# Places of their own for the next stage's first weights at the norms of a two-layer fp32 diffusion step

## Chip, cores and metric

One core of a Trainium2 chip. The time is the device time of one execution in microseconds (us), the median of the runs. Engines: PE multiplies matrices, DVE is the vector engine, ACT the scalar engine, POOL the third elementwise engine, SP only issues transfers.

## What is computed

Two layers over two streams of 128 tokens (stream 0 the context, stream 1 the latent tokens), model width 2048, all in fp32. Each layer is an attention and gating mixer and a feed-forward block, both between two norms:

```python
def ffn_sublayer(x, shift, scale, gate, g_pre, g_post, w_gate, w_up, w_down):
    h = rms_norm(x, g_pre) * (1 + scale) + shift
    f = (jax.nn.silu(h @ w_gate) * (h @ w_up)) @ w_down
    return x + gate * rms_norm(f, g_post)
...
    for l in range(DEPTH):
        sm, cm, gm, sf, cf, gf = modulation(c_ctx, mod_w[l], mod_b[l])
        h = rms_norm(xp, norm_mix_pre[l]) * (1 + cm) + sm
        ...
        xp = xp + gm * rms_norm(merge_heads(o_a, o_b, o_c, w_out[l]), norm_mix_post[l])
        xp = ffn_sublayer(xp, sf, cf, gf, norm_ffn_pre[l], norm_ffn_post[l], w_gate[l], w_up[l], w_down[l])
```

`modulation` is one product of a conditioning vector with `mod_w` (2048 x 12288 for each layer), whose weights have to be read too. Matrices are 2048 x 4608 (`w_in`), 2048 x 2048 (`w_out`), 2048 x 5632 (`w_gate`, `w_up`) and 5632 x 2048 (`w_down`).

## The kernel before

**Pieces and chunks.** Weights come from HBM in pieces of 256 rows x 512 columns (512 KB). A *chunk* is 512 output columns: eight pieces, k = 0 to 15 in blocks of 128 rows, two blocks a piece. All pieces of the program are numbered: the first OUT stage is 72 to 103, the feed-forward stage behind it begins at 104, `w_in` of layer 1 at 368, the second feed-forward stage at 472. For each piece SP issues the transfer to `raw` (`piece`, line 502; once the piece four earlier is split), ACT casts it to `whi` (fp32r), DVE subtracts to `wlo`, and PE multiplies, for each block and stream, `lo x whi`, `hi x wlo`, `hi x whi` of 128 x 512 (12 matmuls a piece, 96 a chunk). `raw`, `whi`, `wlo` are rings of `RING` = 4 places; ACT and DVE may write a place of `whi` and `wlo` when the piece four earlier is used. `ahead` (line 1066) makes them split `LEAD` = 4 pieces in front of PE.

**Stages.** `w_in` in (in), attention, OUT (4 chunks), then three groups of gate/up chunks each with a down stage. Every engine has its own hand-written order, and semaphores tie them.

**The norm** (`turnover`, ACT line 1156, DVE line 1453) stands three times between two stages and, shorter, at the end. The last chunk before it runs its last four pieces for stream 0 first and then for stream 1 (`last=APART` in `dense`, line 747); `half_done` says that stream 0 is complete. Then, for stream 0: ACT copies the last columns out of the bank and squares them, DVE multiplies by the gate row (`gated`), takes the mean, POOL the power, DVE adds to x in four parts, ACT squares those, DVE and POOL make the next norm's factor, DVE normalises blocks of 512 columns to `f`, PE turns each (`turn_x`, four transposes to bank X), ACT or DVE scales by the modulation (`xtmp`), ACT casts to `xt_hi` and DVE subtracts to `xt_lo`. Between these stand the splits of the next stage's first four pieces, which need the ring's places, and stream 1's like work. The first chunk of the next stage (`first=APART`) takes pieces 0 to 3 for stream 0, then for stream 1, then 4 to 7 for both; `TURN_AT` says at which block which turn stands.

**The modulation of later stages** runs beside OUT: `OUT_MODS` gives the pieces after which PE does a *burst* (eight 32-row products over four pieces of `mod_w` in `mraw`, a ring of four), `OUT_FETCH` the pieces behind which SP issues their transfers in pairs. The last burst, ACT's copy of the row, PE's turn of it (`mod_tail`, bank T) and DVE's `norm_vectors` stand in the norm behind OUT. In the feed-forward stages DVE accumulates other vectors piece by piece (`acc`).

Of the kernel before, what the change touches and what calls it, by code (L numbers as in the profile page):

```python
# [56 lines left out]
def turn_order(l, which):  # L57

    if l == which == 0:
        return [(s, b) for b in range(ND) for s in range(2)]  # L60
    return [(0, 0), (0, 1), (1, 0), (1, 1), (0, 2), (1, 2), (0, 3), (1, 3)]


TURN_AT = {((0,), 5): (2, 3), ((1,), 1): (4,), ((1,), 3): (5,), ((1,), 6): (6,), ((0, 1), 8): (7,)}


def scaled_by_act(l, which, i):

    return i % 2 == 1 if l == which == 0 else i in (0, 2, 5, 7)


def edge_of(l, which):
# [209 lines left out]
def build_program(nc, a):  # L282
# [8 lines left out]
    with ExitStack() as ctx:  # L291
# [112 lines left out]
        dve_own = sem("dve_own")  # L404
        pool_own = sem("pool_own")
# [24 lines left out]

        def vec(v, l):
# [21 lines left out]
        def xt_count(l, which):  # L453


            return 16 * l + 8 * (which + 1)
# [281 lines left out]
        def _(pe):  # L738
# [8 lines left out]
            def dense(u, pair, i, hi, lo, nk=KD, ph=0, ready=None, m=None, behind={}, first=0, last=0):  # L747
# [6 lines left out]
                for js in (range(first), range(first, n - last), range(n - last, n)):  # L754
                    together = js.start == first and js.stop == n - last
                    for streams in [(0, 1)] if together else [(0,), (1,)]:
                        for j in js:
                            if streams[0] == 0:
                                pe.wait_ge(lo_ready, u * UNIT + (ph + j + 1))
                            slot = (ph + j) % RING  # L760
                            for kb in range(KB):
# [26 lines left out]
            def products(pair, k, hi, lo, slot, kb, nk=KD, first=0, last=None, streams=(0, 1)):  # L788
                for s in streams:
                    t = slice(s * P, (s + 1) * P)  # L790
                    for n, (xs, ws_) in enumerate([(lo, whi), (hi, wlo), (hi, whi)]):
                        mm = pe.matmul(bank[f"{pair}{s}"][:], xs[:, k, t], ws_[:, slot, kb, :],  # L792
# [4 lines left out]
            def start():  # L797
# [7 lines left out]
                for q in range(ND * QUARTER):  # L805
# [10 lines left out]
                    for kb in range(KB):  # L816
                        mm = products(pair, j * KB + kb, xt_hi, xt_lo, q % RING, kb, first=4 * n, last=4 * n + 3)
# [70 lines left out]
            def pre(l, which):  # L888


                done = xt_count(l, which) - 8

                def ready(k, streams):
# [3 lines left out]
                    if k % 4 == 0:  # L897
                        pe.wait_ge(xt_ready, done + {(0,): 1 + k // 4, (1,): 3 + k // 4, (0, 1): 2 + k // 2}[streams])
# [942 lines left out]
```

## Time and profile before

| what | value |
|---|---|
| runs | 2449.19, 2445.62, 2443.11 us; median 2445.62 |
| profiled execution | 2445.17 us, span 2443.4 |
| PE busy | 2310.0 us, 95% |
| DVE busy | 1578.3 us, 65% |
| ACT busy | 984.4 us, 40% |
| mean granted clock of PE | 0.975 |
| DMA | 609.93 MB, mean 250 GB/s |
| casts and subtractions of pieces | 736 of each, 1050 and 1223 ns |

Busy shares average over stages. The span counts from the first to the last instruction; the 1.8 us between it and the execution's own time lie around it. The three norms lie at 504 to 549, 1276 to 1321 and 1675 to 1720 us, the OUT stages at 412 to 511 and 1582 to 1681.

### The profile page before, as it was taken

To read this page: it belongs to the slowest core of one execution; us is meant where nothing else is said; L and a number is where in the kernel's file an instruction comes from. 1 tells how busy PE (TensorE), PEld (TensorE's weight loads), DVE (VectorE), ACT (ScalarE), POOL (GpSimd) and SP (SyncE) were. 2 spreads that over 40 slices of the span, in tenths; PEclk is the share of its full clock that TensorE was granted. 3 is DMA by queue.
4 is the path that set the end of the run, shared out by engine and by line. 5 is a ranking of instruction groups with operands and counts; after the bars stand their busy time and mean duration, and the time that the engine had idled before them with its cause. 6 is when DMAs were issued, how large, how long until landed. Compare 5 with 4: busy or idle time off the path is not lost.

```text
span 2443.4 us, 28114 instructions
## 1 busy us (share of the span) xinstructions
PE 2310.0 (95%) x10780; PEld 1806.2 (74%) x10780; DVE 1578.3 (65%) x1715; ACT 984.4 (40%) x1253; POOL 67.5 (3%) x97
## 2 busy tenths in 40 slices
PE   4999878989999999999998998798999999999998
PEld 1776645768878888788776885576888888878886
DVE  2555444479988889889886454446888644554455
ACT  2333232454444444334345344335444444434443
POOL 1000020000000000000000102000000000000000
PEclk8999988999999999999999999999999999999999
DMA  8779978858878878788864766885877666656664
GB/s 302 254 281 340 332 274 288 303 193 303 284 254 299 288 265 293 246 280 289 298 198 155 215 208 233 286 300 197 278 268 252 220 196 189 189 182 192 191 221 147
DMA packets 269319, 609.93 MB, mean 250 GB/s; under 512 B 19117, under 2 KB 19297, under 8 KB 267841
## 3 DMA queue, kind: packets, MB, share of 16 engines
q1 hardware_dynamic: 264832, 589.37, 71.5%
q0 software_dynamic: 4352, 18.76, 2.2%
q8 instruction: 86, 1.41, 0.2%
q14 instruction: 49, 0.39, 0.0%
HBM read 603.79 MB, written 5.45 MB: 249 GB/s over the span
## 4 chain that ended last, share of the span: by engine, by line
PE 84%; DMA 6%; DVE 4%; issue 2%; ACT 2%; SPq 0%; POOL 0%; DVEq 0%; POOLq 0%; ACTq 0%
PE bank_A L792 39%; PE bank_B L792 38%; DMA mraw<-in_mod_w 6%; PE bank_M L852 3%; PE bank_X L880 2%; DVE wlo L1362 1%; PE bank_M L841 1%; ACT whi L1094 1%; PE bank_T L872 1%; DVE xtmp L1443 1%; DVE x L1475 0%; DMA raw<-in_w_out 0%; DVE acc L1384 0%; PE bank_M L782 0%; ACT xtmp L1137 0%
## 5 line engine op out<-in xcount | busy, mean ns | idle before, releaser
L1362 DVE TENSOR_TENSOR wlo<-raw,whi 128x1024 fp32r<-128x1024 f32 x736 | 896.7, 1223 | 687.2 <-ACT whi L1094 687.0
L1094 ACT CAST whi<-raw 128x1024 fp32r<-128x1024 f32 x736 | 770.3, 1050 | 1190.8 <-PE bank_A L792 591.3
L792 PE MATMUL bank_A<-whi,xt_lo 128*128 128x512 f32 x1136 | 452.1, 398 | 17.9 <-DVE xt_lo L1413 11.1
L792 PE MATMUL bank_A<-wlo,xt_hi 128*128 128x512 f32 x1136 | 446.8, 393 | 0.0
L792 PE MATMUL bank_A<-whi,xt_hi 128*128 128x512 f32 x1136 | 446.5, 393 | 0.0
L792 PE MATMUL bank_B<-whi,xt_lo 128*128 128x512 f32 x1104 | 433.4, 393 | 0.5 <-issue 0.5
L792 PE MATMUL bank_B<-wlo,xt_hi 128*128 128x512 f32 x1104 | 430.0, 389 | 0.0
L792 PE MATMUL bank_B<-whi,xt_hi 128*128 128x512 f32 x1104 | 429.7, 389 | 0.0
L1384 DVE SCALAR_TENSOR_TENSOR acc<-mraw,cond,acc 128x1024 f32<-128x1024 f32 x300 | 371.2, 1279 | 0.0
L792 PEld LDWEIGHTS bank_A<-whi,xt_lo 128*128 128x128 f32 x1136 | 215.9, 190 | 84.5 <-issue 28.1
L792 PEld LDWEIGHTS bank_A<-whi,xt_hi 128*128 128x128 f32 x1136 | 215.8, 190 | 46.0
L792 PEld LDWEIGHTS bank_B<-whi,xt_lo 128*128 128x128 f32 x1104 | 207.3, 188 | 56.2 <-issue 13.4
L792 PEld LDWEIGHTS bank_A<-wlo,xt_hi 128*128 128x128 f32 x1136 | 215.9, 190 | 43.5
L792 PEld LDWEIGHTS bank_B<-whi,xt_hi 128*128 128x128 f32 x1104 | 207.2, 188 | 43.6
L792 PEld LDWEIGHTS bank_B<-wlo,xt_hi 128*128 128x128 f32 x1104 | 207.3, 188 | 42.0
L792 PE MATMUL bank_A<-whi,ht_lo 128*128 128x512 f32 x352 | 139.2, 395 | 0.7 <-DVE wlo L1362 0.7
L792 PE MATMUL bank_A<-wlo,ht_hi 128*128 128x512 f32 x352 | 138.3, 393 | 0.0
L792 PE MATMUL bank_A<-whi,ht_hi 128*128 128x512 f32 x352 | 137.9, 392 | 0.0
L792 PE MATMUL bank_B<-whi,ht_lo 128*128 128x512 f32 x352 | 137.5, 391 | 0.2 <-DVE wlo L1362 0.2
L792 PE MATMUL bank_B<-wlo,ht_hi 128*128 128x512 f32 x352 | 137.0, 389 | 0.0
L792 PE MATMUL bank_B<-whi,ht_hi 128*128 128x512 f32 x352 | 137.0, 389 | 0.0
L852 PE MATMUL bank_M<-mraw,cond 128*32 128x512 f32 x640 | 93.4, 689 | 30.7 <-DMA mraw<-in_mod_w 30.7
(193 smaller groups left out, 1432.9 us busy)
## 6 DMA issues: line engine op xcount, KB each, us to landing
mraw<-in_mod_w SPq DMA_DIRECT2D x384, 512.0 KB, 6.0
raw<-in_w_gate SPq DMA_DIRECT2D x176, 512.0 KB, 4.4
raw<-in_w_up SPq DMA_DIRECT2D x176, 512.0 KB, 4.4
raw<-in_w_down SPq DMA_DIRECT2D x176, 512.0 KB, 4.8
raw<-in_w_in SPq DMA_DIRECT2D x144, 512.0 KB, 4.7
raw<-in_w_out SPq DMA_DIRECT2D x64, 512.0 KB, 5.8
gate_mix<-gate_rows POOLq DMA_DIRECT2D x4, 1024.0 KB, 6.6
gate_ffn<-gate_rows POOLq DMA_DIRECT2D x4, 1024.0 KB, 9.0
```

What stands on the lines that cost most here:

```text
L792: mm = pe.matmul(bank[f"{pair}{s}"][:], xs[:, k, t], ws_[:, slot, kb, :], start=(k == first and n == 0), stop=(k == (nk - 1 if last is Non ...
L841: mm = pe.matmul(bank["M"][g:g + 32, :], cond[:, 2 * k:2 * k + 32], mraw[:, j % RING, kb, :], start=(k < 4), stop=(k >= KD - 4))
L852: mm = pe.matmul(bank["M"][32 * c:32 * c + 32, :], cond[:, 2 * k:2 * k + 32], mraw[:, ring_piece(m, j + c // 2) % RING, c % 2, :], start=( ...
L872: mm = pe.matmul(bank["T"][:, w * t:w * t + w], mrow[:, t * P:(t + 1) * P], sel[:], start=True, stop=True)
L880: mm = pe.transpose(bank[b][:, n * P:(n + 1) * P], t, ident[:])
L1094: act.copy(whi[:, ph % RING], raw[:, ph % RING]).then_inc(hi_ready, 1)
L1362: dve.tensor_tensor(wlo[:, ph % RING], raw[:, ph % RING], whi[:, ph % RING].bitcast(F32), ALU.subtract).then_inc(lo_ready, 1)
L1384: ins = dve.scalar_tensor_tensor(out=acc[:, h, s, :], in0=w, scalar=c, in1=acc[:, h, s, :], op0=ALU.mult, op1=ALU.add)
L1443: ins = dve.tensor_scalar(xtmp[:, b % 2, s, t, :], bank[bk][:, t * P:(t + 1) * P], scal[:, k, s:s + 1], shift[:, k, s:s + 1], ALU.mult, AL ...
```

## The change

- Places (`EXTRA`, `weights`, `place_free`): the next stage's first four pieces at each norm don't go to the ring but to memory of the feed-forward block that is idle there: halves of `ht_lo` or `ht_hi`, `w_hid` (over `hid` and `sil`) and `w_acc` (over `acc`). The ring's pieces behind them then wait for the piece eight earlier (`last_use`).
- `ahead` splits these four before the norm's chain begins; the four splits inside `turnover` are now those of pieces 4 to 7.
- The first chunk runs all eight pieces for stream 0, then all for stream 1 (`first=UNIT`), with turns in the order of the streams.
- Block 0 of stream 0 is scaled, cast and subtracted in halves (`pre_halves`); ACT scales all blocks but one.
- Behind OUT, squares and gate products read the bank directly, with no copy to `f` first; in all norms the mean stands ahead of the last gate product.
- The modulation's six bursts now all stand inside OUT, with their turn and vectors (`OUT_TAIL`), and `OUT_MODS` and `OUT_FETCH` have new piece numbers.

```diff
-    return [(0, 0), (0, 1), (1, 0), (1, 1), (0, 2), (1, 2), (0, 3), (1, 3)]
-
...
-TURN_AT = {((0,), 5): (2, 3), ((1,), 1): (4,), ((1,), 3): (5,), ((1,), 6): (6,), ((0, 1), 8): (7,)}
+    return [(s, b) for s in range(2) for b in range(ND)]
...
-    return i % 2 == 1 if l == which == 0 else i in (0, 2, 5, 7)
+    return i % 2 == 1 if l == which == 0 else i != 2
...
-OUT_MODS = {3: (0, range(0, 4)), 8: (0, range(4, 8)), 13: (1, range(0, 4)), 19: (1, range(4, 8)), 24: (2, range(0, 4))}
+OUT_MODS = {3: (0, range(0, 4)), 8: (0, range(4, 8)), 12: (1, range(0, 4)), 17: (1, range(4, 8)),
+            21: (2, range(0, 4)), 25: (2, range(4, 8))}
 OUT_FETCH = {4: (0, (0, 1)), 5: (0, (2, 3)), 11: (0, (4, 5)), 12: (0, (6, 7)), 16: (1, (0, 1)), 17: (1, (2, 3)),
-             22: (1, (4, 5)), 23: (1, (6, 7)), 27: (2, (0, 1)), 28: (2, (2, 3)), 31: (2, (4, 5, 6, 7))}
+             20: (1, (4, 5)), 21: (1, (6, 7)), 25: (2, (0, 1)), 26: (2, (2, 3)), 29: (2, (4, 5)), 30: (2, (6, 7))}
+OUT_TAIL = 26
+EDGE_PIECE = [104, 368, 472]
+EXTRA = {g + e: (edge, e) for edge, g in enumerate(EDGE_PIECE) for e in range(RING)}
+
+
+def last_use(g):
+
+    return g - RING if g - RING not in EXTRA else g - 2 * RING
+
+
 MOD_PE = [2, 3, 4, 9, 10]
...
+        with ExitStack() as until_acc:
+            w_acc = sb("w_acc", [P, 4, KB, CH], F32R, until_acc)
...
+        with ExitStack() as until_hid:
+            w_hid = sb("w_hid", [P, 2, KB, CH], F32R, until_hid)
...
+        def weights(g):
+
+            if g not in EXTRA:
+                return whi[:, g % RING], wlo[:, g % RING]
+            edge, e = EXTRA[g]
+            if edge % 2:
+                places = [(tiles(ht_hi, 12), tiles(ht_lo, 12)), (w_hid[:, 0], w_hid[:, 1]),
+                          (w_acc[:, 0], w_acc[:, 1]), (w_acc[:, 2], w_acc[:, 3])]
+            else:
+                places = [(tiles(ht_lo, 0), tiles(ht_lo, 4)), (tiles(ht_lo, 8), tiles(ht_lo, 12)),
+                          (w_hid[:, 0], w_hid[:, 1]), (w_acc[:, 2], w_acc[:, 3])]
+            return places[e]
+
+        def place_free(engine, g):
+
+            if g in EXTRA:
+                if EXTRA[g] in ((1, 2), (1, 3)):
+                    engine.wait_ge(acc_read, MOD_DVE.index(8) + 1)
+            elif g >= RING:
+                engine.wait_ge(w_used, last_use(g) + 1)
...
-            return 16 * l + 8 * (which + 1)
+            return 8 + 9 * (2 * l + which)
...
-                done = xt_count(l, which) - 8
+                done = xt_count(l, which) - 9
...
-                    if k % 4 == 0:
-                        pe.wait_ge(xt_ready, done + {(0,): 1 + k // 4, (1,): 3 + k // 4, (0, 1): 2 + k // 2}[streams])
+                    if streams == (0,) and k in (0, 2):
+                        pe.wait_ge(xt_ready, done + 1 + k // 2)
+                    elif k % 4 == 0:
...
-                    dense(i * 2 + u, "A", i + use["A0"], xt_hi, xt_lo, ready=ready, first=APART if ready else 0)
+                    dense(i * 2 + u, "A", i + use["A0"], xt_hi, xt_lo, ready=ready, first=UNIT if ready else 0)
...
+                        if i == ND - 1 and k == KB * (OUT_TAIL % UNIT + 1):
+                            mod_tail(m + MOD_OUT)
...
+            def pre_halves(l, which):
+
+                bk, n = plan.at[(l, "pre_uses", which)][0]
+                fill_of(bk, n)
+                for k in range(4):
+                    ins = act.activation(xtmp[:, 0, 0, k, :], bank[bk][:, k * P:(k + 1) * P], ACT.Identity,
+                                         scale=scal[:, k, 0:1], bias=shift[:, k, 0:1])
+                    if k == 1:
+                        ins.then_inc(act_own, 1)
+                        act.wait_ge(act_own, edge_of(l, which))
+                        high(xt_hi[:, 0:2, 0:P], xtmp[:, 0, 0, 0:2])
+                ins.then_inc(freed[bk], 1)
+                act.wait_ge(freed[bk], n + 2)
+                high(xt_hi[:, 2:4, 0:P], xtmp[:, 0, 0, 2:4])
+
...
+                def last_square(s):
+                    if which:
+                        act.wait_ge(freed[f"B{s}"], use[f"B{s}"] + 3)
+                        return f_square(s, n)
+                    if s:
+                        act.wait_ge(w_used, u * UNIT + ph + pieces)
+                    else:
+                        act.wait_ge(half_done, edge_of(l, which) + 1)
+                    square(bank[f"B{s}"][:], ssq[:, s, n:n + 1])
...
+                last_square(0)
...
+                ahead = ph + pieces + LEAD
+                split(u, ahead)
+                x_squares(0, range(ND))
+                last_square(1)
...
+                pre_halves(l2, w2)
+                pre_block(l2, w2, 1)
+                x_squares(1, range(2))
...
+                x_squares(1, range(2, ND))
+                pre_block(l2, w2, 3)
+                split(u, ahead + 2)
+                split(u, ahead + 3)
+                for i in range(4, 8):
+                    pre_block(l2, w2, i)
...
-                    ahead(split, u, late=lambda j: pre_late(l, 0, j))
+                    ahead(split, u, LEAD, UNIT - LEAD)
...
+                        ahead(split, u + i, 0, 2)
+                        mod_row(m + MOD_OUT)
+                        ahead(split, u + i, 2, UNIT - 2)
+                        turnover(l, 0, u + i, 0, UNIT, use, split)
...
-                            ahead(split, u, 2 * n * i, 2 * n, leave=LEAD if i == ND - 1 else 0)
+                            ahead(split, u, 2 * n * i, 2 * n)
...
+                mean_square(ssq, sq + 7, slice(0, 1))
                 gated(l, which, ND - 1, 0, sq + 7)
...
+                ahead = ph + pieces + LEAD
+                l2, w2 = l + which, 1 - which
...
+                normal(l2, w2, 2, 3)
...
+                pre_low(l2, w2, 0, range(2))
...
+                add(1, [0])
+                pre_low(l2, w2, 0, range(2, 4))
+                add(1, [1])
+                pre_scale(l2, w2, 2)
+                pre_low(l2, w2, 1)
+                add(1, [2, 3])
+                pre_low(l2, w2, 2)
+                split(u, ahead + 1)
...
+                split(u, ahead + 2)
+                split(u, ahead + 3)
+                normal(l2, w2, 6, 7)
+                for i in range(4, 8):
+                    pre_low(l2, w2, i)
...
+                        ins = dve.tensor_tensor(f[:, i, c], bank[b][:], gate_mix[:, i, c], ALU.mult)
+                        ins.then_inc(freed[b], 1)
...
+                ahead(split, u + ND - 1, 0, 3)
+                mod_cols(m + MOD_OUT)
+                norm_vectors(l, 1)
+                ahead(split, u + ND - 1, 3, UNIT - 3)
+                turnover(l, 0, u + ND - 1, 0, UNIT, split)
```

The order of ACT at the first norm, from the last OUT pieces' casts on; before:

```order
L1094 CAST whi<-raw 128x1024 x4
L1166 COPY f<-bank_B 128x512
L1108 ACTIVATE junk,ssq<-f 128x512
L1094 CAST whi<-raw 128x1024 x2
L1108 ACTIVATE junk,ssx<-x 128x512 x4
L1108 ACTIVATE junk,ssq<-f 128x512
L1123 COPY mrow<-bank_M 128x512
L1094 CAST whi<-raw 128x1024 x2
L1137 ACTIVATE xtmp<-bank_X,shift,scal 128x128 x4
L1112 CAST xt_hi<-xtmp 128x4x128
```

and now:

```order
L1132 CAST whi<-raw 128x1024 x2
L1132 CAST ht_lo<-raw 128x1024 x2
L1132 CAST w_hid<-raw 128x1024
L1132 CAST w_acc<-raw 128x1024
L1146 ACTIVATE junk,ssq<-bank_B 128x512
L1132 CAST whi<-raw 128x1024
L1146 ACTIVATE junk,ssx<-x 128x512 x4
L1146 ACTIVATE junk,ssq<-bank_B 128x512
L1132 CAST whi<-raw 128x1024
L1200 ACTIVATE xtmp<-bank_X,shift,scal 128x128 x2
L1150 CAST xt_hi<-xtmp 128x2x128
L1200 ACTIVATE xtmp<-bank_X,shift,scal 128x128 x2
```

Four more casts (to `ht_lo`, `w_hid`, `w_acc`) stand ahead of the square of the last chunk, its copy is gone, and the row's copy (`mrow`) has moved ahead of them.

The order of DVE at the same place; before:

```order
L1362 TENSOR_TENSOR wlo<-raw,whi 128x1024 x4
L1587 TENSOR_TENSOR f<-f,gate_mix 128x512
L1407 TENSOR_REDUCE msum<-ssq 128x1
L1408 TENSOR_SCALAR ms<-msum 128x1
L1475 SCALAR_TENSOR_TENSOR x<-f,rstd,x 128x512 x4
L1470 COPY f<-bank_B 128x512
L1362 TENSOR_TENSOR wlo<-raw,whi 128x1024
L1407 TENSOR_REDUCE msum<-ssx 128x1
L1408 TENSOR_SCALAR ms<-msum 128x1
L1587 TENSOR_TENSOR f<-f,gate_mix 128x512
L1407 TENSOR_REDUCE msum<-ssq 128x1
L1408 TENSOR_SCALAR ms<-msum 128x1
```

and now:

```order
L1419 TENSOR_TENSOR wlo<-raw,whi 128x1024
L1419 TENSOR_TENSOR ht_lo<-raw,ht_lo 128x1024 x2
L1419 TENSOR_TENSOR w_hid<-raw,w_hid 128x1024
L1419 TENSOR_TENSOR w_acc<-raw,w_acc 128x1024
L1462 TENSOR_REDUCE msum<-ssq 128x1
L1463 TENSOR_SCALAR ms<-msum 128x1
L1640 TENSOR_TENSOR f<-bank_B,gate_mix 128x512
L1527 SCALAR_TENSOR_TENSOR x<-f,rstd,x 128x512 x4
L1419 TENSOR_TENSOR wlo<-raw,whi 128x1024
L1462 TENSOR_REDUCE msum<-ssx 128x1
L1463 TENSOR_SCALAR ms<-msum 128x1
L1484 TENSOR_SCALAR f<-x,rstd 128x512 x2
```

The subtractions of the four early pieces come first, the mean has changed places with the gate product, and the copy to `f` is gone.

The order of SP in the OUT stage, from the pair of `mod_w` pieces behind piece 17 on; before:

```order
L500 DMA mraw<-in_mod_w 128x1024 x2
L506 DMA raw<-in_w_out 128x2x512 x5
L500 DMA mraw<-in_mod_w 128x1024 x2
L506 DMA raw<-in_w_out 128x2x512
L500 DMA mraw<-in_mod_w 128x1024 x2
L506 DMA raw<-in_w_out 128x2x512 x4
L500 DMA mraw<-in_mod_w 128x1024 x2
L506 DMA raw<-in_w_out 128x2x512
L500 DMA mraw<-in_mod_w 128x1024 x2
L506 DMA raw<-in_w_out 128x2x512 x3
L500 DMA mraw<-in_mod_w 128x1024 x4
L506 DMA raw<-in_w_gate 128x2x512 x5
```

and now:

```order
L541 DMA mraw<-in_mod_w 128x1024 x2
L547 DMA raw<-in_w_out 128x2x512 x3
L541 DMA mraw<-in_mod_w 128x1024 x2
L547 DMA raw<-in_w_out 128x2x512
L541 DMA mraw<-in_mod_w 128x1024 x2
L547 DMA raw<-in_w_out 128x2x512 x4
L541 DMA mraw<-in_mod_w 128x1024 x2
L547 DMA raw<-in_w_out 128x2x512
L541 DMA mraw<-in_mod_w 128x1024 x2
L547 DMA raw<-in_w_out 128x2x512 x3
L541 DMA mraw<-in_mod_w 128x1024 x2
L547 DMA raw<-in_w_out 128x2x512
```

The pairs stood behind pieces 17, 22, 23, 27 and 28 and four pieces behind 31; now they stand behind 17, 20, 21, 25, 26 and 29 (and 30, in the row after the last one).

## Rows read from the trace of the kernel before

**Rows 1.** The page: the chain that ended last, by engine.

```profile
PE 84%; DMA 6%; DVE 4%; issue 2%; ACT 2%; SPq 0%; POOL 0%; DVEq 0%; POOLq 0%; ACTq 0%
```

**Rows 2.** The chain of waits in order of time: start, us, what.

```profile
454.14 1.85 PE bank_M L852 x16
...
488.30 1.85 PE bank_M L852 x16
...
504.06 0.60 ACT f L1166
...
549.25 21.76 PE bank_B L792 x96
...
1278.44 0.79 PE bank_T L872 x8
```

**Rows 3.** Timeline of PE, 518 to 549: start, us, engine, line, operation [idle before].

```profile
518.19 0.77 PE L792 MATMUL bank_A<-whi,xt_lo 128*128 128x512 f32 x1 [2.55 <-DVE xt_lo L1413]
518.75 0.63 PE L792 MATMUL bank_A<-wlo,xt_hi 128*128 128x512 f32 x1
519.18 0.63 PE L792 MATMUL bank_A<-whi,xt_hi 128*128 128x512 f32 x1
...
549.09 0.39 PE L792 MATMUL bank_B<-whi,xt_lo 128*128 128x512 f32 x1
```

**Rows 4.** Timeline of ACT, 504 to 517.

```profile
504.68 0.63 ACT L1108 ACTIVATE junk<-f 128x512 f32<-128x512 f32 x1
...
514.88 1.50 ACT L1137 ACTIVATE xtmp<-bank_X,shift,scal 128x128 f32<-128x128 f32 x4 [0.55 <-PE bank_X L880]
516.42 0.62 ACT L1112 CAST xt_hi<-xtmp 128x512 fp32r<-128x512 f32 x1
```

**Rows 5.** Timeline of DVE, 505 to 546.

```profile
505.43 0.69 DVE L1587 TENSOR_TENSOR f<-f,gate_mix 128x512 f32<-128x512 f32 x1 [4.46 <-ACT junk L1108]
...
507.19 2.74 DVE L1475 SCALAR_TENSOR_TENSOR x<-f,rstd,x 128x512 f32<-128x512 f32 x4 [0.68 <-POOL rstd L650]
...
513.12 0.88 DVE L1429 TENSOR_SCALAR f<-x,rstd 128x512 f32<-128x512 f32 x2
...
544.50 1.41 DVE L1381 TENSOR_SCALAR acc<-mraw,cond 128x1024 f32<-128x1024 f32 x2
```

**Rows 6.** Operations of a tile by stretch: 446, 480, 499 to 512, 1274; issue and landing.

```profile
L500 SPq DMA_DIRECT2D mraw<-in_mod_w x1: 430/430/430, 446.6 to 446.6; - x1
...
DMA to landing us min/median/max: 6.7/6.7/6.7
...
L500 SPq DMA_DIRECT2D mraw<-in_mod_w x1: 431/431/431, 480.8 to 480.8; - x1
...
DMA to landing us min/median/max: 7.1/7.1/7.1
...
L1094 ACT CAST whi<-raw x1: 1048/1048/1048, 498.7 to 498.7; 128x1024 fp32r<-128x1024 f32 x1
L1362 DVE TENSOR_TENSOR wlo<-raw,whi x1: 1226/1226/1226, 499.8 to 499.8; 128x1024 fp32r<-128x1024 f32 x1
...
L506 SPq DMA_DIRECT2D raw<-in_w_gate x2: 368/368/368, 501.0 to 511.7; - x2
...
DMA to landing us min/median/max: 3.6/4.0/4.3
...
L506 SPq DMA_DIRECT2D raw<-in_w_in x1: 367/367/367, 1274.1 to 1274.1; - x1
...
DMA to landing us min/median/max: 4.6/4.6/4.6
```

**Rows 7.** Timelines of PE and DVE at the second norm, 1275 to 1321.

```profile
1290.00 0.76 PE L792 MATMUL bank_A<-whi,xt_lo 128*128 128x512 f32 x1 [2.27 <-DVE xt_lo L1413]
...
1320.98 0.39 PE L792 MATMUL bank_B<-whi,xt_lo 128*128 128x512 f32 x1
...
1275.76 0.69 DVE L1468 TENSOR_TENSOR f<-f,bank_B 128x512 f32<-128x512 f32 x1
```

More of the change, by code:

```diff
@@ L786, in dve_vector, with products @@
                     vector_turn(vector_tail(MOD_TAIL[g]), rsel4)
-            def products(pair, k, hi, lo, slot, kb, nk=KD, first=0, last=None, streams=(0, 1)):
+            def products(pair, k, hi, lo, g, kb, nk=KD, first=0, last=None, streams=(0, 1)):
+                w_hi, w_lo = weights(g)
                 for s in streams:
                     t = slice(s * P, (s + 1) * P)
-                    for n, (xs, ws_) in enumerate([(lo, whi), (hi, wlo), (hi, whi)]):
-                        mm = pe.matmul(bank[f"{pair}{s}"][:], xs[:, k, t], ws_[:, slot, kb, :],
+                    for n, (xs, w) in enumerate([(lo, w_hi), (hi, w_lo), (hi, w_hi)]):
+                        mm = pe.matmul(bank[f"{pair}{s}"][:], xs[:, k, t], w[:, kb, :],
                                        start=(k == first and n == 0),
@@ L816, in start @@
                     for kb in range(KB):
-                        mm = products(pair, j * KB + kb, xt_hi, xt_lo, q % RING, kb, first=4 * n, last=4 * n + 3)
+                        mm = products(pair, j * KB + kb, xt_hi, xt_lo, q, kb, first=4 * n, last=4 * n + 3)
                     mm.then_inc(w_used, 1)
@@ L1061, in _, with ahead @@
                               last=APART if g == len(GROUPS) - 1 and i == ND - 1 else 0)
-        def ahead(split, u, ph=0, pieces=UNIT, between=None, leave=0, late=None):
-            for j in range(pieces - leave):
+        def ahead(split, u, ph=0, pieces=UNIT):
+            for j in range(pieces):
                 split(u, ph + LEAD + j)
-                if late:
-                    late(j)
-                if between and j == pieces - 1 - max(leave, 1):
-                    between()
         def past_end(u, ph):
@@ L1091, in split @@
                 act.wait_ge(raw_landed[ph % RING], u * (16 * UNIT // RING) + 16 * (ph // RING + 1))
-                if not (isinstance(u, int) and u * UNIT + ph < RING):
-                    act.wait_ge(w_used, u * UNIT + (ph - RING + 1))
-                act.copy(whi[:, ph % RING], raw[:, ph % RING]).then_inc(hi_ready, 1)
+                place_free(act, u * UNIT + ph)
+                act.copy(weights(u * UNIT + ph)[0], raw[:, ph % RING]).then_inc(hi_ready, 1)
                 if u * UNIT + ph in MOD_ROW:
@@ L1311, in hidden_high @@
                                      four(bank[f"X{s}"][:])).then_inc(ht_hi_ready, 1)
[L1313 removed]
+                    ahead(split, u, 0 if g else LEAD, UNIT if g else UNIT - LEAD)
                     silu(u, 0, True)
@@ L1714, in pair @@
                 def pair(i):
-                    ahead(split, i * 2 + u, late=None if i else lambda j: pre_late(l, 0, j))
+                    ahead(split, i * 2 + u, 0 if i else LEAD, UNIT if i else UNIT - LEAD)
                     read_out(i * 2 + u, i * 2 * CH, "A")
@@ L1760, in _ @@
                     first = 2 * (FFC * l + c0)
-                    ahead(split, u, late=None if g else lambda j: pre_late(l, 1, j))
+                    ahead(split, u, 0 if g else LEAD, UNIT if g else UNIT - LEAD)
                     for i in range(0, n - 1):
@@ L1779, in _ @@
                         else:
-                            ahead(split, u, 2 * n * i, 2 * n, leave=LEAD if i == ND - 1 else 0)
+                            ahead(split, u, 2 * n * i, 2 * n)
                             if i:
```

136 lines of the change are left out of this document (43 added, 93 removed).

## Prediction

> **What bounds the kernel now.** I read the page's chain first: matmuls carry 84% of it [rows 1]. A chunk of 96 dense matmuls takes 21.76 us, 2.72 us for a piece [rows 2], and nothing in the change touches their number. What can move is PE's idle time, so I went through the chain in order of time and stopped where PE is not the link: at the three norms between stages, and in front of the bursts of modulation products. At the first norm the last chunk's stream 0 is complete at 504.06 [rows 2]. The next stage's first dense matmul starts at 518.19 and its second chunk at 549.09 [rows 3]: 14.13 us, then 30.90 us for a chunk whose matmuls need 21.76. The third norm repeats this within 0.1 us. At the second, stream 0 is complete at 1275.76, and the two marks are 1290.00 and 1320.98 [rows 7].
>
> **What goes.** In that 14.13 us PE runs a burst (1.85 us) and the vector's turn (0.79 us where it stands between dense matmuls) [rows 2]. Both move ahead of the mark, into the OUT stage. PE still does them, so this term is a transfer: 2.64 us leave the norm and 2.64 us enter the stage. Reading the bank directly drops ACT's copy. Taking the mean before the gate product hides 0.69 us of gating behind the power: DVE's gating starts at 505.43 and its additions at 507.19, 1.76 us later, of which 0.68 is the wait for POOL [rows 5]. By the new order this is 0.37 (mean) + 0.75 (gate beside power) = 1.12 us.
>
> **What is added to the norm.** ACT and DVE now cast and subtract four pieces of the next stage ahead of the chain. The last of them can be issued only when the last OUT piece is split. In the trace that issue is at 501.0, 3.06 us ahead of the mark, and it landed after 4.3 us; the one issued into an idle queue took 3.6 [rows 6]. The four modulation pieces that queued ahead of it now go out two OUT pieces earlier, so I take 3.6: landed at mark + 0.54. Cast 1.05 [rows 6] gives + 1.6, the square of the last chunk (0.63 and its read-out, about 0.75) [rows 4] + 2.35, DVE's subtraction 1.23 [rows 6] + 2.8. So the chain starts 2 us late, by work that stood behind it before. From there: mean 0.37, gate beside power 0.75, + 3.9; first addition 0.75 and four squares of ACT at 0.82, + 7.95; mean 0.35 and power 0.65, + 8.95; first normalised block 0.45 (0.88 for two [rows 5]), + 9.4; four transposes at the low clock 1.1, + 10.5; half of ACT's scaling (1.50 for four [rows 4]) 0.8, + 11.3; half a cast, between 0.31 (half of 0.62 [rows 4]) and 0.62, taken at 0.4, + 11.7; half a subtraction, likewise 0.4, + 12.15. The first dense matmul starts 12.15 us after the mark in place of 14.13.
>
> **The first chunk.** 96 matmuls are 21.8 us. Twelve run at the low level: starts at 518.75 and 519.18 are 0.43 us apart against 0.23 at the high one [rows 2, 3], 2.4 us. PE had been idle 2.55 us ahead of the first [rows 3]; it will be idle again, so I keep the twelve. Six turns between matmuls cost 0.45 each, 2.7. That is 26.9; the trace's 30.90 holds 4.0 us of waits, since stream 0's first half is followed at once by stream 1's and pieces are split between blocks. With all eight pieces at hand and stream 0 whole, I walked the engines forward: PE waits 0.35 for the seventh piece's subtraction, and 0.85 for stream 1's first block, because the first accumulation (1.41 us on DVE [rows 5]) stands ahead of that block's normalisation. With 0.25 for smaller ones: 28.35. The norm after an OUT stage gives 1.98 + 2.55 - 2.64 = 1.9 us, and two of them 3.8.
>
> **The second norm** is less kind. The down stage's last chunk has six pieces, and the last early one can be issued only after the chunk's own last split, at 1274.1; it takes 4.6 us to land [rows 6], 1278.7. Cast and subtraction end at 1280.95. Gating of chunk 2 (two like that in [rows 5]), the four short vector operations and the last addition, which began at 1275.76 [rows 7], come behind them on DVE: 1.3 + 0.5 + 0.65, 1283.4. The same chain from there (0.75 + 0.37 + 0.75 + 4.03 + 0.6 + 0.65 + 0.45 + 1.13 + 0.8 + 0.45 + 0.4) gives the first dense matmul at 1293.8, 3.8 us later than 1290.00. The chunk then takes 27.5 (no accumulation in it) in place of 30.98. Net +0.3 us.
>
> **The end** has the gate/power exchange twice, 0.62 each by the like of [rows 5]: 1.25 us gained.
>
> **The bursts in OUT.** They move from after pieces 3, 8, 13, 19, 24 and the stage's end to 3, 8, 12, 17, 21, 25, and the transfers for them to behind pieces 17, 21, 26 and 30. A raw piece q is issued when q-4 is split, so after q-8 is used. The burst after 13 was fed behind 17: four pieces of lead. The bursts after 12 (fed behind 17), 21 (26) and 25 (30) have three. In the trace the last transfer for the burst after 13 was issued at 446.6 and landed 6.7 us later, 453.3 [rows 6]; the burst began at 454.14 [rows 2]. One piece earlier its second half wants that data at 454.14 - 2.72 + 0.93 = 452.35: 0.95 short. For the burst after 24 the transfer was issued at 480.8 and took 7.1, 487.9 [rows 6]; the burst began at 488.30 [rows 2]; one piece less gives 486.5, 1.4 short. Chunk 1's boundary gets lighter, so the first takes 0.9, the others 1.4: 3.7 us a stage, 7.4 us in two. Nothing hides them, PE waits. Bounds: 0 (landings as fast as at the norm) and 2.4 a burst (one piece's lead, nearly whole), 0 to 14.4.
>
> What the pair of transfers costs is where a page speaks otherwise. The Trainium skill, "DMA: Bandwidth & Descriptors", section "Anatomy of one DMA — SWDGE (gpsimd) path", fits about 2.0 us plus bytes over 436 GB/s: 3.2 us for 512 KB. The rows' 6.7 and 7.1 are transfers behind others in the queue, the 3.6 at the norm is near the page. By the page's price alone all bursts would be fed in time and the sum would be the first rival's.
>
> **The sum,** against the profiled execution's own 2445.17 us (span 2443.4): -3.8 + 0.3 - 1.25 + 7.4 = +2.65, 2447.8. The median of the runs shown is 2445.62, within half a microsecond; I say 2448.
>
> **Rivals.** (a) *The bursts are fed in time.* The modulation pairs are spread more evenly, so that each queues behind less. Then 7.4 falls away: 2440.5. For it: the 3.6 us landing. Against it: pairs at 446 and 480 were not crowded either. (b) *Fed in time, and the clock is back sooner.* PE's pause at a norm gets shorter; if only half of the twelve matmuls run at the low level and the transposes too, about 1.7 us less at each of three norms: 2435.5. For it: the pause ahead of the first matmul; against: after a 2.55 us pause all twelve were slow. (c) *Slower: every shifted burst waits nearly a whole piece,* 2.4 us for six: 2454.8. It decides the sign beyond measurement above 2.0 us a burst. The longest latency that supports it is 7.1. (d) *The early splits cancel the norm's gain:* the fourth piece lands after 6 us instead of 3.6 at all three norms, the chain starts that much later: 2447.8 + 3.8 = about 2452. The change then does not do what its name says.
>
> **How the numbers follow.** Forecast 0.40, (a) 0.23, (b) 0.15, (c) 0.12, (d) 0.10. A measurement tells about 0.3%, 7.3 us, from no change: faster is below 2438.3, slower above 2453.0. Faster holds (b) and the lower edge of (a): 0.20. Slower holds (c) and the upper edge of (d) and of the forecast: 0.16. Same 0.64. The range leaves out part of (b) and the top of (c): 2436 to 2455.
>
> **What would show it.** In the new profile: PE waits for the modulation tile's transfers in both OUT stages, near 1 us at three bursts each; first dense matmul about 12 us behind the first mark and 18 behind the second; the first chunk 28 us; waits of the first chunk's matmuls for split weights gone but one. No wait at the bursts proves (a); a mark-to-matmul time near 14 proves (d). I would be wrong altogether if a wait came up that the trace doesn't have, for example in the second chunk, whose pieces can be split only as the ring frees in stream 1's pass.

## Result: 11 us slower, and the profile after

The changed kernel takes 2457.24 us (median of 10 runs, 2449.00 to 2463.88); the kernel before, run beside it, 2445.90 (10 runs, 2442.82 to 2451.14). The ratio of the two is 1.0049, 95% interval 1.0036 to 1.0063: slower by 11 us or half a percent, outside the range of the prediction and within 2.5 us of its rival (c).

The profiled execution of the changed kernel took 2461.3 us (span 2459.5), 16.1 us over the span before. Its chain has less of PE and more of DMA than [rows 1]:

```profile
PE 81%; DMA 8%; DVE 5%; ACT 2%; issue 2%; SPq 1%; POOL 1%; POOLq 0%; DVEq 0%; ACTq 0%
L893 PE MATMUL bank_M<-mraw,cond 128*32 128x512 f32 x640 | 92.3, 674 | 44.2 <-DMA mraw<-in_mod_w 44.1
```

The last row is the page's group of all modulation products: duration, mean ns, and 44.2 us of idle time ahead of them, nearly all of it waiting for transfers. The same row of the kernel before has 30.7 us, none of it inside an OUT stage:

```profile
L852 PE MATMUL bank_M<-mraw,cond 128*32 128x512 f32 x640 | 93.4, 689 | 30.7 <-DMA mraw<-in_mod_w 30.7
```

I cut both spans at five marks that each chain of waits shows: the first dense matmul of each OUT stage and the start of the second chunk behind each norm. The stretches add up to the spans, and so their differences to 16.1.

| stretch | before | after | difference | predicted |
|---|---|---|---|---|
| start to first OUT stage | 411.59 | 411.29 | -0.3 | 0 |
| first OUT stage and first norm | 137.66 | 145.32 | +7.7 | +1.8 |
| feed-forward and second norm | 771.89 | 772.45 | +0.6 | +0.3 |
| `w_in` and attention of layer 1 | 261.12 | 262.52 | +1.4 | 0 |
| second OUT stage and third norm | 137.69 | 145.05 | +7.4 | +1.8 |
| rest, with the end | 723.45 | 722.87 | -0.6 | -1.25 |

The loss lies in the OUT stages. These are the waits there, from the timeline of PE (start, us, operation, idle time before it and what ended it), first stage, then second:

```profile
440.63 1.07 PE L893 MATMUL bank_M<-mraw,cond 128*32 128x512 f32 x8 [0.61 <-DMA mraw<-in_mod_w]
...
456.01 1.07 PE L893 MATMUL bank_M<-mraw,cond 128*32 128x512 f32 x8 [2.20 <-DMA mraw<-in_mod_w]
...
487.11 1.06 PE L893 MATMUL bank_M<-mraw,cond 128*32 128x512 f32 x8 [2.23 <-DMA mraw<-in_mod_w]
...
502.87 1.06 PE L893 MATMUL bank_M<-mraw,cond 128*32 128x512 f32 x8 [1.01 <-DMA mraw<-in_mod_w]
...
1635.24 1.07 PE L893 MATMUL bank_M<-mraw,cond 128*32 128x512 f32 x8 [1.55 <-DMA mraw<-in_mod_w]
...
1666.40 1.07 PE L893 MATMUL bank_M<-mraw,cond 128*32 128x512 f32 x8 [2.30 <-DMA mraw<-in_mod_w]
...
1681.78 1.06 PE L893 MATMUL bank_M<-mraw,cond 128*32 128x512 f32 x8 [2.17 <-DMA mraw<-in_mod_w]
```

They are 6.05 and 6.02 us, where 3.7 a stage was predicted; the bursts of before in [rows 2] run their sixteen products in one go. Each stands in the middle of a burst, ahead of its second half. Two of them cost more than themselves: the dense matmuls behind the wait run at the lower of PE's two clock levels for a while.

```profile
488.10 0.64 PE L833 MATMUL bank_A<-whi,xt_lo 128*128 128x512 f32 x1
488.54 0.63 PE L833 MATMUL bank_A<-wlo,xt_hi 128*128 128x512 f32 x1
...
491.53 0.48 PE L833 MATMUL bank_A<-whi,xt_hi 128*128 128x512 f32 x1
491.85 0.40 PE L833 MATMUL bank_A<-whi,xt_lo 128*128 128x512 f32 x1
```

The starts are 0.43 us apart up to 491.5 and 0.23 to 0.32 from there. By the chain of waits those twelve took 4.55 us; twelve behind another stalled burst took 2.98:

```profile
441.69 2.98 PE bank_B L833 x12
...
488.17 4.55 PE bank_A L833 x12
```

### The profile page after: what moved, and what is told of

The parts are those of the page before. It is cut to its first block, busy times and chain, and to the rows that moved or that the text cites. A ratio compares the mean times of both kernels' runs of the same rounds, so it can differ in the third digit from the quotient of the medians.

```text
span 2459.5 us, 28085 instructions
## 1 busy us (share of the span) xinstructions
PE 2312.7 (94%) x10780; PEld 1808.9 (74%) x10780; DVE 1561.8 (64%) x1674; ACT 994.1 (40%) x1284; POOL 67.5 (3%) x97
## 4 chain that ended last, share of the span: by engine, by line
PE 81%; DMA 8%; DVE 5%; ACT 2%; issue 2%; SPq 1%; POOL 1%; POOLq 0%; DVEq 0%; ACTq 0%
PE bank_A L833 38%; PE bank_B L833 36%; DMA mraw<-in_mod_w 7%; PE bank_M L893 3%; PE bank_X L921 2%; DVE wlo L1419 2%; PE bank_M L882 1%; ACT whi L1132 1%; PE bank_T L913 1%; DMA raw<-in_w_out 0%; ACT junk L1146 0%; SPq L541 0%; DVE x L1527 0%; DVE xt_lo L1468 0%; DVE acc L1439 0%
## 5 line engine op out<-in xcount | busy, mean ns | idle before, releaser
L1419 DVE TENSOR_TENSOR wlo<-raw,whi 128x1024 fp32r<-128x1024 f32 x724 | 881.8, 1223 | 708.3 <-ACT whi L1132 707.6
L1132 ACT CAST whi<-raw 128x1024 fp32r<-128x1024 f32 x724 | 758.6, 1050 | 1201.9 <-PE bank_A L833 600.7
L833 PE MATMUL bank_A<-whi,xt_lo 128*128 128x512 f32 x1088 | 430.5, 396 | 4.2 <-DVE xt_lo L1468 3.7
L833 PE MATMUL bank_A<-wlo,xt_hi 128*128 128x512 f32 x1088 | 426.9, 392 | 0.0
L833 PE MATMUL bank_A<-whi,xt_hi 128*128 128x512 f32 x1088 | 426.2, 392 | 0.0
L833 PEld LDWEIGHTS bank_A<-whi,xt_lo 128*128 128x128 f32 x1088 | 206.3, 190 | 66.6 <-issue 22.5
L833 PEld LDWEIGHTS bank_A<-whi,xt_hi 128*128 128x128 f32 x1088 | 206.2, 190 | 43.7
L833 PEld LDWEIGHTS bank_A<-wlo,xt_hi 128*128 128x128 f32 x1088 | 206.3, 190 | 41.9
L833 PE MATMUL bank_A<-whi,ht_lo 128*128 128x512 f32 x352 | 138.8, 394 | 0.7 <-DVE wlo L1419 0.7
L833 PE MATMUL bank_A<-wlo,ht_hi 128*128 128x512 f32 x352 | 137.7, 391 | 0.0
L893 PE MATMUL bank_M<-mraw,cond 128*32 128x512 f32 x640 | 92.3, 674 | 44.2 <-DMA mraw<-in_mod_w 44.1
```

The costliest lines, as they stand in the source:

```text
L833: mm = pe.matmul(bank[f"{pair}{s}"][:], xs[:, k, t], w[:, kb, :], start=(k == first and n == 0), stop=(k == (nk - 1 if last is None else l ...
L893: mm = pe.matmul(bank["M"][32 * c:32 * c + 32, :], cond[:, 2 * k:2 * k + 32], mraw[:, ring_piece(m, j + c // 2) % RING, c % 2, :], start=( ...
L1132: act.copy(weights(u * UNIT + ph)[0], raw[:, ph % RING]).then_inc(hi_ready, 1)
L1419: dve.tensor_tensor(lo, raw[:, ph % RING], hi.bitcast(F32), ALU.subtract).then_inc(lo_ready, 1)
```

## Experiments

Theory after the result: the bursts with three pieces of lead are the whole loss, by their waits, and by the clock where a wait lowers it. Rivals: the bursts cost what the prediction said and the rest is in the norms; or traffic and the number of restarts cost, not the lead. All times below are medians beside runs of the kernel before on the same chip, 2445.53 for the first four kernels, 2445.86 for the last four. Beside the changed kernel it was 2445.90, so I subtract medians across the three series; by the scatter of the runs such a difference is known to about 4 or 5 us.

### The burst table alone, in the kernel before

```diff
-OUT_MODS = {3: ..., 8: ..., 13: (1, range(0, 4)), 19: (1, range(4, 8)), 24: (2, range(0, 4))}
+OUT_MODS = {3: ..., 8: ..., 12: (1, range(0, 4)), 17: (1, range(4, 8)), 21: (2, range(0, 4)), 25: (2, range(4, 8))}
...
-                mod(m + MOD_OUT, range(UNIT // 2, UNIT))
```

and `OUT_FETCH` as in the changed kernel.

> The kernel before with one part of the change: its modulation bursts in the OUT stages run after pieces 3, 8, 12, 17, 21 and 25 with the transfers moved to match; norms, chunk order and places are the old ones. In the changed kernel's trace the first OUT stage holds 6.05 us of waits for the modulation tile in five places, a chunk part at the low clock after one of them (4.55 us for twelve matmuls in place of 2.72) and four restarts at 2.98 us a piece in place of 2.72. Theory (the short leads and the clock that PE loses after such a wait are the whole loss): 6.05 + 1.8 + 1.0 = 8.9 us a stage, and 1.85 us more, because the last burst leaves a place at the norm where it was hidden: 2 x 10.75 = +21.5, about 2467 us. Rival (bursts cost the 3.7 us a stage of the prediction, the rest of the loss is in the norms): 2 x (3.7 + 1.85) = +11, 2457 us, with waits near 1 us at the bursts and no piece at the low clock.

Measured: 2461.72 us, ratio 1.0063 (1.0039 to 1.0087), +16.2. That lies between the two figures. The profiled execution, with span 2466.1, is 22.7 us over that of before. Its chain has the waiting transfers (these are of the first OUT stage) and a wait that the changed kernel avoids, PE waiting 3.0 us for ACT's copy of the row, since `mod_tail` still stands behind the stage:

```profile
446.76 7.50 DMA mraw<-in_mod_w
...
477.47 6.65 DMA mraw<-in_mod_w
...
491.64 7.50 DMA mraw<-in_mod_w
```

No low-clock piece followed a wait in the first OUT stage, the waits there being 4.7 us. In the second they are 5.6 us, and the last, 2.90 us, was followed by one: the 48 matmuls behind it took 12.73 us, the same 48 in the first stage 11.12.

```profile
1682.62 12.73 PE bank_B L794 x48
```

So a table of numbers, with none of the places or orders in the change's name, makes the kernel before slower by 16 us. The profile is with the theory and the medians lie midway, so this run alone doesn't decide between them; the later ones do.

### Bursts in pairs, evenly spread

```diff
+OUT_MODS = {q: (n // 4, (2 * n % 8, 2 * n % 8 + 1)) for n, q in enumerate([2, 4, 6, 8, 10, 12, 14, 17, 19, 21, 24, 25])}
+OUT_FETCH = {q: (n // 4, (2 * n % 8, 2 * n % 8 + 1)) for n, q in enumerate([4, 5, 10, 12, 14, 16, 18, 20, 22, 25, 27, 29])}
```

> The changed kernel, its six bursts of four modulation pieces cut into twelve of two, after pieces 2, 4, 6, 8, 10, 12, 14, 17, 19, 21, 24 and 25, each pair's transfer behind the piece that follows the pair two before it: every lead is four or five pieces, as many products as before. Theory: the waits in both OUT stages go, and with them the piece at the low clock: 2 x (6.05 + 1.8) = -16, 2441 us. Rival one (bursts cost 3.7 a stage): -7.4, 2450. Rival two (it is not the lead but the traffic: the latencies grow as transfers are spread, or twelve restarts of 0.25 us cost what the waits did): 2455 or more, with waits still there.

Measured: 2447.20 us, ratio 1.0004 (0.9987 to 1.0021), 10.0 less than the changed kernel. Both OUT stages have no wait for `mraw` at all (138.8 and 138.3 us with their norms, in place of 145.3 and 145.1). The -16 fell short by 6. A restart of dense matmuls behind a burst costs about 0.3 us whether the burst is of two or four pieces; with six more a stage that is 3.6 of the 6, and the rest is within the scatter. The rows are

```profile
423.69 1.00 PE bank_M L891 x8
424.69 5.67 PE bank_A L831 x24
```

where 24 matmuls need 5.44 and eight products 0.93.

### The last early pieces split behind the chain

```diff
+def held_back(l, which):
+    return 2 if which else 1
...
-                split(u, ahead)
+                rest = [ahead + e for e in range(-held_back(l, which), RING)]
+                split(u, rest[0])
                 x_squares(0, range(ND))
                 last_square(1)
-                split(u, ahead + 1)
+                split(u, rest[1])
```

and the like on DVE, where `rest[0]` stands behind `add(0)` and `rest[1]` behind `add(1, [1])`; the last chunk's `ahead` splits one or two pieces fewer.

> The changed kernel, but the early pieces that land last (the fourth at the norms after OUT, the third and fourth at the norm after the down stage) are split behind the last square and behind the first additions of the norm's chain in place of ahead of it. Places, transfers and products are the same. Theory (the splits hold the chain): the chain starts 2.0 us sooner at the first and third norm (mean at 518.97 in the trace, possible at about 516.9) and 4.3 us sooner at the second (last addition at 1289.15, possible at 1284.8), all of it kept since PE wants those pieces only 3 to 4 us into the chunk: -8.3, 2449 us. Rival (what is taken from the front comes back as waits of the first chunk for its split pieces or blocks): 2455 or more, and a first chunk longer than 28.4 us.

Measured: 2447.66 us, ratio 1.0008 (0.9991 to 1.0024), 9.6 less than the changed kernel. At the first norm stream 0 is complete at 508.53 (the end of its 36 matmuls) and the first dense matmul starts at 518.59, 10.06 us later in place of 12.22; the first chunk takes 28.20 in place of 28.43, so nothing is given back:

```profile
500.25 8.28 PE bank_B L838 x36
...
518.59 2.69 PE bank_A L838 x6
...
546.79 21.76 PE bank_B L838 x96
```

From the last down chunk to the second chunk behind the second norm it is 91.15 us in place of 93.74: 2.6 of the 4.3. The first dense matmul comes 61.4 us behind that down chunk's start in place of 65.9, the 4.3 expected; but the chunk takes 29.7 us (1288.33 to 1318.05) in place of 27.8, which is the rival, at this one norm. At the third norm mark to matmul is 10.07 us in place of 11.95. The three give 2.2 + 2.6 + 1.9 = 6.7. The profile also has shorter waits in OUT, 5.0 and 4.2 us, which the edit doesn't aim at, 2.8 us less than in the changed kernel; whether the other 2.9 of the 9.6 is that or scatter stays open.

### Both together

The two edits above in one kernel.

> The edits of the two kernels ahead of this one together: bursts in pairs, late pieces split behind the norm's chain. Theory: both gains add up, -16 and -8.3: 2433 us, 13 us faster than the kernel before. Rival (one gain hides the other, or the second is given back in the first chunk): 2441 or more.

Measured: 2435.28 us, ratio 0.9962 (0.9944 to 0.9981): -22.0 against the changed kernel, where 10.0 and 9.6 had been measured singly. They add up within the scatter, and the kernel is faster than the one before.

### One table altered: four pieces of lead

```diff
-             20: (1, (4, 5)), 21: (1, (6, 7)), 25: (2, (0, 1)), 26: (2, (2, 3)), 29: (2, (4, 5)), 30: (2, (6, 7))}
+OUT_FETCH = {4: (0, (0, 1)), 5: (0, (2, 3)), 11: (0, (4, 5, 6, 7)), 16: (1, (0, 1, 2, 3)), 20: (1, (4, 5, 6, 7)),
+             25: (2, (0, 1, 2, 3)), 29: (2, (4, 5, 6, 7))}
```

Nothing else of the changed kernel is touched.

> The changed kernel with one table altered: all four modulation pieces for a burst are issued behind one weight piece, the eighth after the burst before, so that each burst has four pieces of lead (the one after 17 five); bursts, places and norms as changed. Theory (the lead of three pieces is what the bursts pay for, not their number or size): nearly all of the waits in OUT and the low-clock piece go, without the six extra restarts a stage that bursts in pairs had (0.3 us each, 3.6 in all; that kernel took 2447.2): about 2443 to 2445 us. Rival (four transfers in a row land later by 0.8 us for each that stands ahead, and hold the weight pieces behind them): waits near 1 us stay at four bursts a stage, 2450 us or more.

Measured: 2442.17 us, ratio 0.9988 (0.9977 to 1.0000): 15.1 less than the changed kernel. This is the cleanest price of the bursts' lead, though its profiled execution (2450.29) was the slowest of its twelve. In that one the two stretches of OUT and norm take 139.6 and 137.6 us, together 13.2 less than in the changed kernel's. The waits of the first OUT stage are 0.6 us in one place, the second has none:

```profile
PE bank_M L893 <- DMA mraw<-in_mod_w: 0.6, 1, 0.6
```

although each transfer takes longer from issue to landing, four standing in a row (those issued at 454.4 and 454.9):

```profile
L541 SPq DMA_DIRECT2D mraw<-in_mod_w x2: 430/677/924, 454.4 to 454.9; - x2
...
DMA to landing us min/median/max: 9.0/9.4/9.8
```

The rival was right that they land later, and wrong on what it costs: 0.6 us in one place of two stages.

### One table altered: two pieces of lead

`OUT_FETCH` of the changed kernel with its last ten keys each one higher.

> The changed kernel with each of the ten moved transfers of the modulation pieces issued one weight piece later (leads of two in place of three; four in place of four or five at the others less one). Theory (a burst waits for landing less lead, and landing is near 7.9 us whatever the lead): each of four stalled bursts a stage waits 2.72 us more, the one with four pieces of lead begins to wait 2 us: 2 x (4 x 2.72 + 2) = +26, 2483 us, less what shorter queues give. Rival (what the transfer queues behind is the weight pieces, so a later issue lands sooner and the wait is capped near 2.3 us): under 2468 us.

Measured: 2497.86 us, ratio 1.0214 (1.0195 to 1.0234): +40.6 for one piece less of lead, where +26 was expected, and -15.1 for one piece more. The rival's cap falls. The first OUT stage with its norm takes 164.5 us. Idle time there:

```profile
PE bank_M L893 <- DMA mraw<-in_mod_w: 18.2, 8, 2.7
```

That is 12.1 over the changed kernel's 6.05, near the 13 expected. Most of the other 7 us of the stage's +19.2 is the clock, of which I had expected nothing more. The eight stalls are, in order, 2.41, 2.12, 2.72, 2.15, 1.79, 2.68, 1.65 and 2.67 us. Three of them, each the second stall within one burst, are followed by a burst at the low level (1.93 or 1.94 us for eight products in place of 1.07) and dense matmuls 0.43 us apart. The three bursts took 2.6 us longer for it and the dense matmuls behind them 4.3, where the changed kernel lost 1.6 in this stage; 1.2 us more went at the stage's entry (13.20 us for its first 48 matmuls in place of 12.01, see the last section). The rows of the first of the three:

```profile
456.76 1.93 PE L893 MATMUL bank_M<-mraw,cond 128*32 128x512 f32 x8 [2.72 <-DMA mraw<-in_mod_w]
458.62 0.80 PE L833 MATMUL bank_B<-whi,xt_lo 128*128 128x512 f32 x1
459.22 0.63 PE L833 MATMUL bank_B<-wlo,xt_hi 128*128 128x512 f32 x1
459.64 0.63 PE L833 MATMUL bank_B<-whi,xt_hi 128*128 128x512 f32 x1
```

Stretches by granted clock (the number ahead of the DMA share), behind two of these stalls:

```profile
456.76:465.91 9.15, 9.15 (x33) 6.11 (x34) 1.22 (x1) 1.05 (x1) 0.00 (x0) 0.72 0.16 60
514.60:521.07 6.47, 6.47 (x23) 3.93 (x23) 0.00 (x0) 0.59 (x1) 0.00 (x0) 0.59 0.29 108
```

The Trainium skill, "TensorE: Matmul & The Clock Gate", section "HAM oscillation — how this bites in real kernels", describes this: a wait for DMA between stretches of matmuls returns PE to its cold clock, and each stretch then pays for warming up on top of the wait; the waits of its example are longer than any of these. This trace agrees for three of the eight stalls; the five others, up to 2.41 us, were followed by full speed. In the second stage it agrees for four of eight (2.71, 2.71, 2.73 and 2.73 us).

### Four pieces of lead, late splits

The last altered table and `held_back` together.

> The early issue of the modulation pieces and the late split of the last early pieces together (bursts of four, leads of four). Theory: -9.6 (held back, as measured against the changed kernel) and -13: 2434 to 2436 us, level with the pairs and held-back kernel (2435.3) or 2 us under it, since twelve restarts are saved and four transfers in a row cost a part of that. Rival: waits near 1 us stay at the bursts: 2441 or more.

Measured: 2433.32 us, ratio 0.9956 (0.9942 to 0.9970). The lowest of all: 24 us under the changed kernel, 12.5 under the one before. The 2 us under the pairs and held-back kernel are within the scatter. The stretches are 134.5 and 133.2 us for OUT and norm, against 137.7 before. The second norm keeps the wait that holding back brings:

```profile
PE bank_A L838 <- DVE wlo L1426: 1.8, 1, 1.8
```

### Old norms, bursts in pairs

The kernel before with the pairs' two tables and nothing left at the stage's end. Against the pairs kernel it lacks the new norms, places, chunk order and end, and nothing else.

> The kernel before (its norms, chunk order and places) with the twelve bursts of two in OUT, fed with four pieces of lead, none left at the stage's end. It differs from the pairs kernel (2447.2 us) by the new norms, places, chunk order and end alone. By the traces: the last burst leaves its hidden place, 1.85 us, and six more restarts of 0.3: 2 x 3.65 = +7.3, 2453 us; the new norms would be worth about 6 us. By the prediction's own terms the chain and first chunk after OUT are worth 2 x 4.5 us, the end 1.25 and the second norm costs 0.3: this kernel would be 10 us slower than the pairs kernel, 2457. Rival (the new norms bring nothing): 2447.

Measured: 2455.75 us, ratio 1.0044 (1.0027 to 1.0060). The pairs kernel is 8.5 us faster. By this the rival (the new norms bring nothing) falls. Between the 6 of the expectation and the 10 of the prediction's own terms the runs don't decide. In the profiled executions the two stretches of OUT and norm are 145.8 and 142.7 us, against 138.8 and 138.3 in the pairs kernel; 2.3 of the 11.4 between them lie at the entry of the stages (last section). From the last down chunk to the second chunk behind the second norm the pairs kernel takes 2.0 us more, 94.5 against 92.6.

## Why the prediction was wrong

**The chain and chunk behind OUT: right.** Stream 0 complete to first dense matmul was predicted 12.15 us, the first chunk 28.35. At the first norm the mark (stream 0 complete) is 515.96 (510.52 and 24 matmuls, 5.44 us):

```profile
507.68 2.84 PE bank_B L833 x12
...
512.93 3.61 DMA raw<-in_w_gate
...
528.18 2.90 PE bank_A L833 x6
...
556.61 3.40 PE bank_B L833 x15
```

12.22 and 28.43 us. The fourth piece landed in 3.61 us (3.6 assumed), which ends rival (d) as it was put. That rival was right about one thing, though: the early splits do hold the chain. The prediction had priced that at 2 us, and it is 2.2 and 1.9, by the held-back kernel.

**The second norm: right mechanism, 0.9 us more than predicted.** Last down chunk to second chunk is 93.74 us against 92.56, +1.2 in place of +0.3. Its first dense matmul comes 4.5 us later than before, 3.8 predicted, and the chunk takes 27.8 in place of 27.5:

```profile
1280.80 4.35 DMA raw<-in_w_in
...
1287.39 1.30 DVE f L1637 x2
...
1301.25 2.90 PE bank_A L833 x6
```

**The end: 0.6 of 1.25 gained.** Gate and power now lie side by side twice, but POOL's power took 0.93 us in the last of them, against 0.56 before.

**The term that failed is the bursts': 7.4 predicted, 15.1 measured** (changed kernel less four-pieces-of-lead kernel), at the upper bound of 14.4 within the scatter. The mechanism was right, PE waiting for transfers whose lead had become three pieces; the size of the waits was wrong, and what they do to the clock was put at nothing. The identity of the stalled bursts was right (after 12, 21, 25), and so was their lead. In the changed kernel the last pair for the burst after 12 was issued at 448.02, and PE wanted it at 456.01 - 2.20 = 453.81: 5.79 us. The prediction's own numbers were 446.6 and 452.35: 5.75. For the burst after 21 it is 479.11 to 484.88, 5.77. With the 0.14 us from landing to product, a burst with three pieces of lead waits its landing time + 0.14 - 5.8. What was wrong:

- *The landing times.* I took 6.7 and 7.1 us from single transfers of before [rows 6] as though they went with the burst. They are 7.86, 7.86 and 6.67 in the first stage, 7.21, 7.95 and 7.83 in the second:

```profile
448.02 7.86 DMA mraw<-in_mod_w
...
479.11 7.86 DMA mraw<-in_mod_w
...
496.06 6.67 DMA mraw<-in_mod_w
```

  By this they give 2.2, 2.2, 1.0 and 1.55, 2.3, 2.2; with 0.61 at the burst after 8 that is 12.1 us for two stages, 4.7 over the forecast. The pair of 448.02 stood behind a weight piece that itself took 6.3 us; before, the one issued at 445.7 took 4.8. The rows, after and then before:

```profile
L547 SPq DMA_DIRECT2D raw<-in_w_out x1: 378/378/378, 447.1 to 447.1; - x1
...
DMA to landing us min/median/max: 6.3/6.3/6.3
```

```profile
L506 SPq DMA_DIRECT2D raw<-in_w_out x1: 379/379/379, 445.7 to 445.7; - x1
...
DMA to landing us min/median/max: 4.8/4.8/4.8
```

  So what stood ahead of the pair landed 1.5 us later, and I had priced each pair as if it met the backlog of before. Part of it is scatter: in the first OUT stage the kernel with the burst table alone has 7.50, 6.65 and 7.50 with the same spacing, and the held-back kernel 7.00, 7.33 and 7.68. The twelve together have a mean of 7.4, which by the same sum is 1.75 us a burst and 5.3 a stage, against 3.7. How much of the 7.4 comes from packing the same 24 transfers into fewer pieces wasn't tried.
- *What a wait does besides waiting.* The twelve matmuls at 488.17 took 1.57 us more than those at 441.69, and those at 1682.84 (4.54) likewise: 3.1 us. The prediction discussed the clock only at the norms. With the 12.1 us of waits, less the 0.6 that the kernel with four pieces of lead keeps, that is 14.6 of the 15.1.
- *The bound.* "One piece's lead, nearly whole" for three bursts a stage left out that the burst after 8, with four pieces, can be late (0.61 us), and left out the clock (3.1 us), so 14.4 was no real bound; the profiled execution has 12.1 + 3.1 = 15.2 us.

**The rivals.** Rival (c), 2454.8, had the right size for nearly the right reason (2.20, 2.23, 1.01 and 1.55, 2.30, 2.17 us at the six shifted bursts, the clock on top); I gave it 0.12 with the words that the longest latency that supports it is 7.1. [rows 6] are a handful of transfers and no maximum; the same trace of before has this pair, issued at the stage's end:

```profile
L500 SPq DMA_DIRECT2D mraw<-in_mod_w x2: 429/574/718, 490.2 to 490.7; - x2
...
DMA to landing us min/median/max: 8.7/9.1/9.5
```

Rival (a), the bursts fed in time, is the kernel with one table altered: 2442.17 for a forecast of 2440.5. The forecast's other terms thus stand within 2 us, and the 0.9 of the second norm and 0.65 of the end, missed above, are 1.55 of the 1.7. Rival (b) has no support. The first chunk's granted clock (the number ahead of the DMA share) is 0.92, and was 0.91, in these stretches of after and before:

```profile
528.18:556.61 28.43, 27.72 (x121) 21.97 (x122) 18.31 (x30) 21.44 (x46) 0.55 (x1) 0.92 0.30 97
```

```profile
518.19:549.09 30.90, 28.17 (x120) 21.81 (x121) 24.86 (x43) 17.14 (x32) 0.55 (x1) 0.91 0.55 178
```

Rival (d) was priced wrongly besides: a piece landing 2.4 us later at three norms would be 7.2 us, 2455.0, and not the 3.8 that were added.

A transfer's price was the place where the Trainium skill spoke otherwise ("DMA: Bandwidth & Descriptors", section "Anatomy of one DMA — SWDGE (gpsimd) path": about 2.0 us plus bytes over 436 GB/s, 3.2 us for 512 KB), in a fit to transfers issued by gpsimd, where these are issued by SP. The trace agrees within half a microsecond where nothing stood ahead, the fourth early piece at 3.61 us. The pair behind a weight piece took 7.1 and 7.9, and there the measurement decides: a lead is set by these.

```profile
L541 SPq DMA_DIRECT2D mraw<-in_mod_w x2: 433/450/467, 447.5 to 448.0; - x2
...
DMA to landing us min/median/max: 7.1/7.5/7.9
```

## What to carry to other kernels

A prefetch has a lead (from issue to need) and a landing time behind everything queued ahead of it. When a change moves the consumer one step earlier, work out the lead from the trace and hold it against the longest landing under load, not against one row: here one step less cost 15 us and the next 41, and one table that issues a step earlier gave the first back. Where a norm or another serial chain has a fixed start, put no work ahead of it that waits for a transfer still under way: moving one or two such splits behind the chain's first steps gave 9.6 us, 6.7 of them seen in the norms.

## What the runs showed of the hardware

**A stall of PE near 2 us may or may not lower its clock.** The length alone doesn't decide. In the changed kernel 2.20 and 2.30 us were followed by full speed, 2.17 and 2.23 by a stretch at the low level. With the late splits 2.03 us in the first OUT stage was followed by full speed, and 1.91 us in the second by the low level:

```profile
1650.69 1.07 PE L898 MATMUL bank_M<-mraw,cond 128*32 128x512 f32 x8 [1.91 <-DMA mraw<-in_mod_w]
...
1651.75 4.55 PE bank_A L838 x12
```

All eight waits in the OUT stages of 2.67 us or more were followed by the low level. Six of them stood behind an earlier stall of 1.65 to 2.12 us in the same burst, but 2.71 us (two pieces of lead, at 1638.73) and the 2.90 us of the burst table alone had no stall ahead of them in their burst. The longest alone that was followed by full speed is 2.41 us. What decides between 1.9 and 2.4 us stays open.

**The same instructions behind the same pause took different times.** Every kernel here has one pause in the middle of the feed-forward stage of layer 0, followed by the same 84 matmuls. In the profiled executions they took between 20.43 and 21.90 us, where 84 at full speed need 19.0:

```profile
985.48 20.48 PE bank_A L792 x84
```

The row is of the kernel before; this one is of the pairs kernel:

```profile
983.87 21.90 PE bank_A L831 x84
```

The entry of OUT is like it. The first 48 matmuls of its first stage took 11.1 us in the kernel before and in the one with four pieces of lead and late splits, in profiled executions, 12.01 in the changed one (12.39 in the second stage) and 12.42 with the burst table alone, whose program up to that point is that of before. About 2 us of the 16.1 in the table above are this and not the change, and with the last eight products ahead of the second OUT stage (1.94 us at the low level in place of 1.07, part of the +1.4 in the table) it is about 3; the medians' 11.3 is the better figure for what the change costs.
